# The residual's rounding, squaring and low part, one unit later in the output projection of a decoder step

## The chip, the cores and the metric

The kernel runs on one core of one Trainium2 chip. The metric is the device time of one launch in microseconds (us). Before the change it is 1759.76 us, the median of three runs (1758.87 to 1760.71 us).

## What is computed

The reference is one layer of a hybrid decoder for a prompt of 1024 tokens and 8 single-token requests, 1032 tokens in all. The change lies in its tail:

```python
def finish(x, ret_y, nsa_y, w_o, ln_post_mix, ln_pre_ffn, w_up, w_down, ln_post_ffn):
    mix = jnp.concatenate([ret_y, nsa_y], -1) @ w_o
    h = x + rmsnorm(mix, ln_post_mix)
    f = jnp.square(jax.nn.relu(rmsnorm(h, ln_pre_ffn) @ w_up)) @ w_down
    return h + rmsnorm(f, ln_post_ffn)
```

All tensors are float32. Features lie on the 128 partitions (8 tiles of features, `kt`), tokens in the free dimension, in three chunks of 344.

## The kernel before, in words

**Products in three parts.** Each float32 operand of a large product is split into a rounded part (`hi`, made by ScalarE with a copy) and the rest (`lo`, made by VectorE with a subtraction). A product is then three matmuls: hi by hi, hi by lo, lo by hi.

**Units.** `stage_tail` begins with 42 units, numbered `u`. The first 24 are the output projection `w_o`: for each of three token chunks, eight output tiles. The next 18 are the first part of `w_up`: six output tiles for each chunk. One unit is 24 matmuls of 128x344 at L2414, and writes one of three PSUM banks. Its weights (512 KB) come by a DMA that SyncE issues (L2232), `round_hi` on ScalarE makes `tail_hi` (L2534), and `reduce_lo` on VectorE makes `tail_lo` (L2753). Two buffers hold the split weights, so the rounding for unit u+1 waits until TensorE has finished unit u-1.

**What follows a chunk.** While the units of the next chunk run, the finished chunk goes through the rest of `h` and the start of the second norm. `place_of(u)` gives the chunk `k` and the slot `j` (0 to 7) for that side work. Slots 1 and 2 turn the chunk's sums of squares into a factor per token. From slot 2 on, feature tiles are taken as this table says:

```python
        SLOT_KT = {2: (0, 1), 3: (2, 3), 4: (4,), 5: (5,), 6: (6, 7), 7: ()}
```

For each feature tile, in this order:
- TensorE turns the tile of `x` into feature order (`turn_x`, three small matmuls at L2362), before the unit's own matmuls. It waits until the residual two tiles back has been added, because two PSUM banks hold the turned tiles.
- VectorE scales the projection (L2804) and adds the turned `x` (L2808). This is `residual`, and its result is `h`, in the tile `mixed_then_h`.
- GpSimd issues a DMA that stores the tile of `h` (L2283).
- ScalarE rounds `h` times the norm's gain into `act_hi` (L2572) and squares `h` into one of five buffers `h_squares` (L2575). Both are `normed_hi`.
- VectorE makes the low part `act_lo` (L2813, `normed_lo`), which needs `act_hi`.

TensorE adds up four squares at a time (`sum_h`, L2351): tiles 0 to 3 in slot 5 of the same chunk, tiles 4 to 7 in slot 1 of the next.

**The order on each engine** is written out by hand as one loop over `u` per engine, and each engine runs its instructions in that order. For one unit:
- ScalarE: `round_hi(u + 1)`; the side work of slots 1 to 3; the square and the copy of unit u-1's result (L2547, L2548), or the square of the `w_up` result (L2552); `normed_hi` for the slot's tiles; `scale_x`, a scaling of an earlier chunk's `h` (L2583), in units 16 to 27 and 32 to 35.
- VectorE: `reduce_lo(u + 1)`; the side work; the sum of squares of unit u-1 (L2769), or, ahead of `reduce_lo`, the relu of the `w_up` result (L2777); `residual` for the slot's tiles; `normed_lo` for the same tiles.
- SyncE: the weight loads in order, and behind each from unit 28 on the store of a `w_up` result.

After the 42 units TensorE runs the rest of the feed-forward layer (L2469 and L2519), to the end of the kernel.

Of the kernel before, what the change touches and what calls it, by code (L numbers as in the profile page):

```python
# [1914 lines left out]
def stage_tail(nc, m, ps, io, h_rows, f_forms, f_last):  # L1915
# [6 lines left out]
    with Stage(nc, "tail") as ctx:  # L1922
# [110 lines left out]
        SLOT_KT = {2: (0, 1), 3: (2, 3), 4: (4,), 5: (5,), 6: (6, 7), 7: ()}  # L2033
# [15 lines left out]
        def place_of(u):  # L2049

            if KT <= u < 4 * KT:
                return u // KT - 1, u % KT
            if 4 * KT <= u < NU:
                return 3, u - 4 * KT + 1
            return None, None

        def y_place_of(u):
            return (u // KT - 1, u % KT) if u >= KT else (None, None)
# [274 lines left out]
        def _(pe):  # L2333
            ones = m.c("ones")

            def token_totals(sums, at):

                for j in range(4):
                    last = pe.matmul(ps[0:SUB, 6, at + j:at + j + 1], sums[:, j * SUB:(j + 1) * SUB], ones[:, 0:1], start=True, stop=True,  # L2339
                                     skip_group_check=True)  # L2340
                return last

            def spread_out(out, d):
                return pe.matmul(out, ones[0:SUB, :], d[:].rearrange("p a n -> p (a n)"), start=True, stop=True, skip_group_check=True)

            def sum_h(grp):
                pe.wait_ge(h_squared, 4 * grp + 4)
                if grp % 2 == 0 and grp:
                    pe.wait_ge(h_copied, grp // 2)
                for i in range(4):  # L2350
                    last = pe.matmul(ps[32 * i:32 * i + 32, 7, 0:TN], ones[:, 0:32], hsq[(4 * grp + i) % 5][:], start=(grp % 2 == 0),  # L2351
                                     stop=(grp % 2 == 1), skip_group_check=True)
                last.then_inc(h_summed, 1)

            def turn_x(c, kt):
                g = KT * c + kt
                if kt == 0:
                    pe.wait_ge(x_loaded[c], 48 if c == 2 else 32)
                if g >= 2:
                    pe.wait_ge(h_ready, g - 1)  # L2360
                for t, n in enumerate(PIECES):
                    last = pe.transpose(ps[:, 3 + g % 2, t * P:t * P + n], x[X_SLOT[c]][0:n, t, kt * P:(kt + 1) * P], m.c("ident")[0:n, 0:n])  # L2362
                last.then_inc(x_turned, 1)

            def behind_chunk(k, j):
                if j == 1:
                    if k < 3:
                        if k >= 2:
                            pe.wait_ge(rstd_ready, k - 1)
                        pe.wait_ge(summed, 7 * (k + 1))  # L2370
                        token_totals(acc[k % 2], 0).then_inc(totals, 1)
                    if k:
                        sum_h(2 * k - 1)
                if j == 2:
                    if k < 3:
                        pe.wait_ge(diagonal, k + 1)
                        if k:
                            pe.wait_ge(normed, KT * k)
                        spread_out(ps[:, 5, 0:TN], diag).then_inc(spread, 1)
                    if k:  # L2380
                        pe.wait_ge(h_copied, k)
                        token_totals(h_part, 4).then_inc(h_totals, 1)
                if j == 3 and k:
                    pe.wait_ge(h_diagonal, k)
                    spread_out(ps[:, 6, 64:64 + TN], h_diag).then_inc(h_spread, 1)
                if k < 3:
                    if j == 5:
                        sum_h(2 * k)
                    for kt in SLOT_KT[j] if j >= 2 else ():
                        turn_x(k, kt)  # L2390

            for u, (what, n, c) in enumerate(tiles):
                k, j = place_of(u)
# [108 lines left out]
            for u in range(NL):  # L2502
                c, n = divmod(u, KT)
                k, j = y_place_of(u)
# [24 lines left out]
        def _(act):  # L2529
            def round_hi(p):  # L2530
                act.wait_ge(raw_loaded[raw_slot[p]], 16 * raw_use[p])
                if p >= 2:
                    act.wait_ge(unit_done, p - 1)
                act.activation(whi[p % 2][:], wraw[raw_slot[p]][:], ACT.Copy).then_inc(hi_ready, 1)  # L2534

            def split(n):
                c = n // 4
                for kts in mix_parts(n):
                    act.activation(m.hi[:, kts, chunk(c)], m.mixT[:, kts, chunk(c)], ACT.Copy).then_inc(mix_hi, 1)

            def evacuate(u):
                what, n, c = tiles[u]
                if what == "o":
                    act.wait_ge(unit_done, u + 1)
                    if n >= 3:
                        act.wait_ge(summed, 7 * c + n - 2)
                    act.activation(msq[n % 2][:] if n else acc[c % 2][:], ps[:, u % 3, 0:TN], ACT.Square).then_inc(squared, 1)  # L2547
                    act.activation(hT[:, n, chunk(c)], ps[:, u % 3, 0:TN], ACT.Copy).then_inc(o_evacuated, 1)  # L2548
                else:
                    k = u - NO  # L2550
                    act.wait_ge(evacuated, k + 1)
                    act.activation(f[k % 3][:], f[k % 3][:], ACT.Square).then_inc(f_squared, 1)  # L2552
# [24 lines left out]
            def scale_x(n):  # L2577

                c, kt = divmod(n, KT)
                act.wait_ge(n_lo, n + 1)  # L2580
                act.wait_ge(h_squared, n + 1)
                act.wait_ge(h_stored[c], 16 * KT)
                act.activation(hT[:, kt, chunk(c)], hT[:, kt, chunk(c)], ACT.Copy, scale=m.lnT[:, 16 + kt:17 + kt]).then_inc(scaled, 1)  # L2583
# [91 lines left out]
            for u in range(NU + 1):  # L2675
                if u in head_ends:
                    evacuate(u - 1)
                if u and u + 1 < NU:
                    round_hi(u + 1)
                k, j = place_of(u)  # L2680
                if k is not None:
                    behind_chunk(k, j)
                if u and u not in head_ends:
                    evacuate(u - 1)
                if u < 8:
                    split(4 + u)
                if k is not None and k < 3 and j >= 2:
                    for kt in SLOT_KT[j]:
                        normed_hi(k, kt)
                if 2 * KT <= u < NO:  # L2690
                    scale_x(u - 2 * KT)
                if NO <= u < NO + 4:
                    scale_x(KT + 2 * (u - NO))
                    scale_x(KT + 2 * (u - NO) + 1)
                if 4 * KT <= u < 4 * KT + 4:
                    for kt in X_SCALES[u - 4 * KT]:
                        scale_x(2 * KT + kt)
                if u in (38, 40):
                    x_hi_of((u - 38) // 2)
                if u == NU - 2:  # L2700
                    left_hi_of(0)
                if u == NU - 1:
                    for at in range(1, LEAD):
                        left_hi_of(at)
                if u == NU:
                    x_hi_of(2)
# [42 lines left out]
        def _(dve):  # L2749
# [260 lines left out]
            for u in range(NU + 1):  # L3010
                early = u in head_ends or u > NO + 1
                if early:
                    evacuate(u - 1)
                if u and u + 1 < NU:
                    reduce_lo(u + 1)
                k, j = place_of(u)
                if k is not None:
                    behind_chunk(k, j)
                if u and not early:
                    evacuate(u - 1)  # L3020
                if u < 8:
                    split(4 + u)
                if k is not None and k < 3 and j >= 2:
                    for kt in SLOT_KT[j]:
                        residual(k, kt)
                    for kt in SLOT_KT[j]:
                        normed_lo(k, kt)
                for n, q in X_PARTS.get(u, ()):
                    x_difference(n, q)
                if u == 39:  # L3030
                    first_sums()
                if u == 40:
                    x_lo_of(0, 0)
                    x_lo_of(0, 1)
                    left_lo_of(0)
                if u == NU - 1:
                    for at in range(1, LEAD):
                        left_lo_of(at)
                if u == NU:
                    x_lo_of(1, 0)  # L3040
                    x_lo_of(1, 1)
# [108 lines left out]
```

## Time and profile before

| | |
|---|---|
| median of three runs | 1759.76 us |
| the profiled execution's own time | 1759.33 us |
| its span in the trace | 1757.6 us |
| TensorE busy | 1637.6 us, 93% of the span |
| VectorE busy | 1063.5 us, 61% |
| ScalarE busy | 694.0 us, 39% |
| granted TensorE clock, mean | 0.975 |

The time of a run counts from launch to end, the span from the first to the last instruction in the trace; they differ by 1.7 us. The trace says for every instruction when it began, how long it took, and, in square brackets, how long its engine had stood idle before it and what ended that. Overlapping instructions of one engine are both shown in full, so the distance between two starts can be shorter than the duration.

### The profile page before, as it was taken

What the parts mean: (1) busy time and instruction counts of PE and PEld (TensorE: products, weight loads), DVE (VectorE), ACT (ScalarE), POOL (GpSimd) and SP (SyncE); (2) the same over time, 40 slices, a digit from 0 to 9 for tenths busy, and PEclk for the clock granted to TensorE, in tenths of its full rate; (3) what the DMA queues carried; (4) which work ended last, traced back from release to release, by engine and by line L of the source; (5) the groups of instructions that cost most, each with busy time, mean ns of one, the idle gap of its engine ahead of it and who ended that gap; (6) DMA issues with size and microseconds to landing.
All of it is one profiled execution on the core that took longest, in us unless ns stands there. A gap on an engine that the chain in (4) does not pass through costs nothing. (4 is left out here: it accounts for less than half of the span.)

```text
span 1757.6 us, 31453 instructions
## 1 busy us (share of the span) xinstructions
PE 1637.6 (93%) x12256; PEld 1453.7 (83%) x12256; DVE 1063.5 (61%) x1841; ACT 694.0 (39%) x1270; POOL 212.9 (12%) x305
## 2 busy tenths in 40 slices
PE   4999999997889778999998989999999999999997
PEld 4989989897784566655556988999999999999997
DVE  5556352121115536777876666877776788787566
ACT  5223322211001127666655665633333453433343
POOL 1000000012533220000000110032222000000011
PEclk9999999999899889999999999999999999999998
DMA  8111111142885340000006546534343743543464
GB/s 303 49 38 50 37 50 40 29 120 82 221 223 169 113 132 1 1 1 0 1 1 172 151 138 190 155 121 151 133 145 139 277 170 127 187 146 121 126 173 159
DMA packets 206838, 204.05 MB, mean 116 GB/s; under 512 B 15325, under 2 KB 175666, under 8 KB 203106
## 3 DMA queue, kind: packets, MB, share of 16 engines
q1 hardware_dynamic: 170930, 154.33, 28.3%
q0 software_dynamic: 12720, 37.21, 6.9%
q10 hardware_dynamic: 23040, 10.50, 2.3%
q8 instruction: 98, 1.61, 0.4%
q14 instruction: 50, 0.41, 0.1%
HBM read 163.27 MB, written 42.89 MB: 117 GB/s over the span
## 5 line engine op out<-in xcount | busy, mean ns | idle before, releaser
L2469 PE MATMUL psum<-right_hi,left_hi 128*128 128x258 f32 x1088 | 307.6, 283 | 3.3 <-issue 2.8
L2469 PE MATMUL psum<-right_hi,left_lo 128*128 128x258 f32 x1088 | 307.4, 283 | 0.0
L2469 PE MATMUL psum<-right_lo,left_hi 128*128 128x258 f32 x1088 | 307.0, 282 | 0.0
L235 PE MATMUL psum<-act_hi,whi 128*128 128x344 f32 x648 | 213.4, 329 | 4.0 <-DVE act_lo L408 4.0
L2469 PEld LDWEIGHTS psum<-right_hi,left_hi 128*128 128x128 f32 x1088 | 205.6, 189 | 3.7 <-issue 2.9
L235 PE MATMUL psum<-act_hi,wlo 128*128 128x344 f32 x648 | 206.9, 319 | 0.0
L235 PE MATMUL psum<-act_lo,whi 128*128 128x344 f32 x648 | 206.8, 319 | 0.0
L2469 PEld LDWEIGHTS psum<-right_lo,left_hi 128*128 128x128 f32 x1088 | 205.7, 189 | 0.0
L2469 PEld LDWEIGHTS psum<-right_hi,left_lo 128*128 128x128 f32 x1088 | 205.6, 189 | 0.0
L235 PEld LDWEIGHTS psum<-act_hi,whi 128*128 128x128 f32 x648 | 121.8, 188 | 11.4 <-DVE act_lo L408 4.4
L235 PEld LDWEIGHTS psum<-act_lo,whi 128*128 128x128 f32 x648 | 121.8, 188 | 0.4
L235 PEld LDWEIGHTS psum<-act_hi,wlo 128*128 128x128 f32 x648 | 121.8, 188 | 0.0
L2414 PE MATMUL psum<-act_hi,tail_hi 128*128 128x344 f32 x328 | 107.1, 326 | 5.2 <-issue 5.2
L2612 ACT ACTIVATE left_hi<-down_weights 128x512 fp32r<-128x512 f32 x84 | 52.9, 632 | 133.9 <-PE psum L2469 130.7
L2414 PE MATMUL psum<-act_hi,tail_lo 128*128 128x344 f32 x328 | 104.8, 319 | 0.0
L2414 PE MATMUL psum<-act_lo,tail_hi 128*128 128x344 f32 x328 | 104.6, 319 | 0.0
L1738 ACT ACTIVATE att_pT<-psum 128x512 f32<-128x512 f32 (+2 forms) x152 | 76.0, 539 | 42.1 <-PE psum L1667 40.3
L1667 PE MATMUL psum<-const,att_p 128*128 128x128 f32 x528 | 76.8, 280 | 13.0 <-ACT att_pT L1738 12.1
L2469 PE MATMUL psum<-act_hi,left_lo 128*128 128x258 f32 x312 | 88.1, 282 | 0.0
L2469 PE MATMUL psum<-act_hi,left_hi 128*128 128x258 f32 x312 | 88.1, 282 | 0.0
L2469 PE MATMUL psum<-act_lo,left_hi 128*128 128x258 f32 x312 | 88.0, 282 | 0.0
L2854 DVE TENSOR_TENSOR left_lo<-down_weights,left_hi 128x512 fp32r<-128x512 f32 x84 | 57.8, 688 | 43.4 <-ACT left_hi L2612 43.4
(441 smaller groups left out, 3622.3 us busy)
## 6 DMA issues: line engine op xcount, KB each, us to landing
hidden_forms<-pair_out SPq DMA_DIRECT2D x84, 258.0 KB, 2.4
right_raw<-hidden_forms SPq DMA_DIRECT2D x21, 1032.0 KB, 5.0
wraw<-in_w_in SPq DMA_DIRECT2D x27, 512.0 KB, 3.7
pair_raw<-in_w_up SPq DMA_DIRECT2D x13, 1024.0 KB, 5.5
down_weights<-in_w_down SPq DMA_DIRECT2D x12, 1024.0 KB, 7.9
last_raw<-in_w_down SPq DMA_DIRECT2D x24, 512.0 KB, 3.9
tail_raw<-in_w_o SPq DMA_DIRECT2D x23, 512.0 KB, 4.5
tail_raw<-in_w_up SPq DMA_DIRECT2D x18, 512.0 KB, 4.5
```

Of the source, the lines that this page charges most:

```text
L235: last = pe.matmul(out, w[:, kt, :], x[:, kt, :], start=(kt == 0 and n == 0), stop=(kt == KT - 1 and n == 2))
L1667: last = pe.transpose(ps[:, 4 + n % 2, (x - a) * P:(x - a + 1) * P], p[k % 3][:, block_cols(i, x)], m.c("ident"))
L1738: act.activation(pT[(t // R) % 2][:, a:b, t % R, :], ps[:, 4 + n % 2, 0:(b - a) * P].rearrange("p (a n) -> p a n", n=P), ACT.Copy).then_in ...
L2414: last = pe.matmul(ps[:, u % 3, 0:TN], wt[:, kt, :], xt[:, kt, cols], start=(kt == 0 and i == 0), stop=(kt == KT - 1 and i == 2))
L2469: last = pe.matmul(ps[:, first_bank(at) + e, 0:HT // 2], wt[:, kt, :], xt[:, kt, cols], start=(opens and kt == 0 and i == 0), stop=(kt == ...
L2612: act.activation(left_hi[at % SLOTS][:], left_source(at), ACT.Copy).then_inc(form_hi, 1)
L2854: dve.tensor_tensor(left_lo[at % SLOTS][:], left_source(at), left_hi[at % SLOTS][:].bitcast(F32), ALU.subtract).then_inc(form_lo, 1)
```

## The change

Three engines' loops are touched. In the chunk's side work `normed_hi` on ScalarE and `normed_lo` on VectorE take the tiles of the slot before (slot j handles `SLOT_KT[j - 1]`), so each follows its tile's `residual` by one unit. `residual` stays where it is. On TensorE the first `sum_h` of a chunk moves from slot 5 to slot 6. No instruction is added or removed, and no DMA is moved.

```diff
@@ block.tensor, behind_chunk
                 if k < 3:
-                    if j == 5:
+                    if j == 6:
                         sum_h(2 * k)
                     for kt in SLOT_KT[j] if j >= 2 else ():
                         turn_x(k, kt)
@@ block.scalar
                 if u < 8:
                     split(4 + u)
-                if k is not None and k < 3 and j >= 2:
-                    for kt in SLOT_KT[j]:
+                if k is not None and k < 3 and j >= 3:
+                    for kt in SLOT_KT[j - 1]:
                         normed_hi(k, kt)
@@ block.vector
                 if k is not None and k < 3 and j >= 2:
                     for kt in SLOT_KT[j]:
                         residual(k, kt)
-                    for kt in SLOT_KT[j]:
+                    for kt in SLOT_KT[j - 1] if j > 2 else ():
                         normed_lo(k, kt)
```

ScalarE, first chunk, from slot 2 into slot 3 (`tail_hi` is the rounded weight of the next unit; a minus is a row that stood there before, a plus one that stands there now):

```order
 L2547 ACTIVATE mix_squares_13194<-psum 128x344
 L2548 ACTIVATE mixed_then_h<-psum 128x344
-L2572 ACTIVATE act_hi<-mixed_then_h,lnT 128x344
-L2575 ACTIVATE h_squares_13179<-mixed_then_h 128x344
-L2572 ACTIVATE act_hi<-mixed_then_h,lnT 128x344
-L2575 ACTIVATE h_squares_13180<-mixed_then_h 128x344
 L2534 ACTIVATE tail_hi_13189<-tail_raw_13185 128x1024
 L2547 ACTIVATE mix_squares_13193<-psum 128x344
 L2548 ACTIVATE mixed_then_h<-psum 128x344
 L2572 ACTIVATE act_hi<-mixed_then_h,lnT 128x344
+L2575 ACTIVATE h_squares_13179<-mixed_then_h 128x344
+L2572 ACTIVATE act_hi<-mixed_then_h,lnT 128x344
```

The four instructions that need `h` of this slot stood ahead of the next weight's rounding; now the rounding and the evacuation of one more unit come first.

VectorE, second chunk, from the last residual of slot 2 to the end of slot 3. Before:

```order
L2808 TENSOR_TENSOR mixed_then_h<-mixed_then_h,psum 128x344
L2813 SCALAR_TENSOR_TENSOR act_lo<-mixed_then_h,lnT,act_hi 128x344 x2
L2753 TENSOR_TENSOR tail_lo_13191<-tail_raw_13185,tail_hi_13189 128x1024
L2769 TENSOR_TENSOR mix_square_sums_13195<-mix_square_sums_13195,mix_squares_13193 128x344
L2804 SCALAR_TENSOR_TENSOR mixed_then_h<-mixed_then_h,lnT,psum 128x344
L2808 TENSOR_TENSOR mixed_then_h<-mixed_then_h,psum 128x344
L2804 SCALAR_TENSOR_TENSOR mixed_then_h<-mixed_then_h,lnT,psum 128x344
L2808 TENSOR_TENSOR mixed_then_h<-mixed_then_h,psum 128x344
L2813 SCALAR_TENSOR_TENSOR act_lo<-mixed_then_h,lnT,act_hi 128x344 x2
```

With the change:

```order
L2808 TENSOR_TENSOR mixed_then_h<-mixed_then_h,psum 128x344
L2753 TENSOR_TENSOR tail_lo_13191<-tail_raw_13185,tail_hi_13189 128x1024
L2769 TENSOR_TENSOR mix_square_sums_13195<-mix_square_sums_13195,mix_squares_13193 128x344
L2804 SCALAR_TENSOR_TENSOR mixed_then_h<-mixed_then_h,lnT,psum 128x344
L2808 TENSOR_TENSOR mixed_then_h<-mixed_then_h,psum 128x344
L2804 SCALAR_TENSOR_TENSOR mixed_then_h<-mixed_then_h,lnT,psum 128x344
L2808 TENSOR_TENSOR mixed_then_h<-mixed_then_h,psum 128x344
L2813 SCALAR_TENSOR_TENSOR act_lo<-mixed_then_h,lnT,act_hi 128x344 x2
```

The pair of low parts ahead of `tail_lo` is gone from this place; the pair at the end is now that of slot 2. The totals per chunk are the same.

## Rows read from the trace of the kernel before

**Rows 1.** Busy time by stretch, the numbers from the start of the span

```profile
core 0: us, PE busy (x) PEld busy (x) DVE busy (x) ACT busy (x) POOL busy (x), PEclk, DMA share, GB/s
984.00:1104.00 120.00, 111.01 (x744) 103.35 (x743) 81.58 (x136) 72.25 (x142) 14.87 (x27) 1.00 0.54 162
1104.00:1134.00 30.00, 30.00 (x193) 30.00 (x192) 25.51 (x30) 17.46 (x25) 0.00 (x0) 1.00 0.51 148
1500.00:1700.00 200.00, 200.00 (x1559) 199.78 (x1558) 146.37 (x196) 78.97 (x93) 8.08 (x15) 1.00 0.46 149
```

**Rows 2.** Who waited for whom, 984 to 1104 us: total, times, longest

```profile
DVE tail_lo L2753 <- ACT tail_hi L2534: 31.0, 23, 3.6
ACT act_hi L2572 <- DVE mixed_then_h L2808: 29.6, 15, 2.2
...
PE psum L2362 <- DVE mixed_then_h L2808: 6.1, 7, 1.8
ACT tail_hi L2534 <- DMA tail_raw<-in_w_up: 5.7, 3, 2.8
...
PE psum L2414 <- issue: 2.9, 2, 1.9
```

**Rows 3.** ScalarE's timeline: start, duration, instruction, idle time before it

```profile
1039.08 0.58 ACT L2572 ACTIVATE act_hi<-mixed_then_h,lnT 128x344 fp32r<-128x344 f32 x1 [2.14 <-DVE mixed_then_h L2808]
1039.57 0.48 ACT L2575 ACTIVATE h_squares<-mixed_then_h 128x344 f32<-128x344 f32 x1
1039.95 0.57 ACT L2583 ACTIVATE mixed_then_h<-mixed_then_h,lnT 128x344 f32<-128x344 f32 x1
1040.42 1.04 ACT L2534 ACTIVATE tail_hi<-tail_raw 128x1024 fp32r<-128x1024 f32 x1
1041.37 0.43 ACT L2547 ACTIVATE mix_squares<-psum 128x344 f32<-128x344 f32 x1
1041.71 0.44 ACT L2548 ACTIVATE mixed_then_h<-psum 128x344 f32<-128x344 f32 x1
1044.28 0.58 ACT L2572 ACTIVATE act_hi<-mixed_then_h,lnT 128x344 fp32r<-128x344 f32 x1 [2.13 <-DVE mixed_then_h L2808]
```

**Rows 4.** VectorE's timeline in the same unit

```profile
1041.57 1.23 DVE L2753 TENSOR_TENSOR tail_lo<-tail_raw,tail_hi 128x1024 fp32r<-128x1024 f32 x1 [1.29 <-ACT tail_hi L2534]
1042.71 0.51 DVE L2769 TENSOR_TENSOR mix_square_sums<-mix_square_sums,mix_squares 128x344 f32<-128x344 f32 x1
1043.13 0.56 DVE L2804 SCALAR_TENSOR_TENSOR mixed_then_h<-mixed_then_h,lnT,psum 128x344 f32<-128x344 f32 x1
1043.73 0.51 DVE L2808 TENSOR_TENSOR mixed_then_h<-mixed_then_h,psum 128x344 f32<-128x344 f32 x1
1044.90 0.58 DVE L2813 SCALAR_TENSOR_TENSOR act_lo<-mixed_then_h,lnT,act_hi 128x344 fp32r<-128x344 f32 x1 [0.65 <-ACT act_hi L2572]
```

**Rows 5.** TensorE's timeline around a slot boundary without a wait

```profile
983.90 0.40 PE L2414 MATMUL psum<-act_hi,tail_hi 128*128 128x344 f32 x1
...
987.75 0.76 PE L2362 MATMUL psum<-const,x_rows_again 128*128 128x128 f32 x6
988.30 0.41 PE L2414 MATMUL psum<-act_hi,tail_hi 128*128 128x344 f32 x1
```

**Rows 6.** TensorE's timeline at the two longest waits of the stretch

```profile
1042.00 0.46 PE L2362 MATMUL psum<-const,x_rows_again 128*128 128x128 f32 x3
1044.30 0.52 PE L2362 MATMUL psum<-const,x_rows_again 128*128 128x128 f32 x3 [1.85 <-DVE mixed_then_h L2808]
1044.61 0.41 PE L2414 MATMUL psum<-act_hi,tail_hi 128*128 128x344 f32 x1
...
1054.32 0.39 PE L2414 MATMUL psum<-act_hi,tail_hi 128*128 128x344 f32 x1 [1.93 <-issue]
```

**Rows 7.** DMA issues by line, 1054 to 1134 us: KB each, median us to landing

```profile
tail_raw<-in_w_up SPq DMA_DIRECT2D x16, 512.0 KB, 4.5
```

**Rows 8.** The slowest landing of a `w_up` tile: SyncE's issue, ScalarE's rounding

```profile
1089.36 0.37 SPq L2232 DMA_DIRECT2D tail_raw<-in_w_up  x1
...
1095.40 1.06 ACT L2534 ACTIVATE tail_hi<-tail_raw 128x1024 fp32r<-128x1024 f32 x1 [1.69 <-DMA tail_raw<-in_w_up]
```

**Rows 9.** TensorE's waits from 1134 us to the end

```profile
PE psum L2481 <- DVE mlp_out L3004: 4.6, 2, 3.8
PE psum L2469 <- issue: 2.8, 1, 2.8
PE psum L2339 <- DVE y_square_sums L2984: 1.7, 1, 1.7
PE psum L2469 <- DVE pair_out L2918: 0.6, 1, 0.6
```

## The prediction, as put on record before the changed kernel ran

> **What bounds the kernel now.** I read the busy times by stretch first. From 1104 us to 1700 us TensorE hardly pauses, and the last such stretch has it busy for all of 200.00 us [rows 1]. Where TensorE is the bound, only time that TensorE gives up can be won. The stretch of the change, 984 to 1104 us, is different: TensorE is busy for 111.01 of 120.00 us, at a granted clock of 1.00, the 2.4 GHz level. VectorE (81.58 us) and ScalarE (72.25 us) have more than a quarter of it free [rows 1]. So about 9 us of TensorE idle time lie here, while no engine is full.
>
> The waits name the cause [rows 2]. TensorE waited 7 times for a residual (6.1 us) and twice for a split weight (shown as "issue", 2.9 us): 9.0 us in nine waits. In the same stretch VectorE waited 31.0 us for ScalarE's rounded weight, and ScalarE 29.6 us for VectorE's residual. Two engines that wait for each other that long, both unfilled, run in a ring.
>
> The timelines show the ring's length for a slot with one feature tile in the second chunk: from one `act_hi` at 1039.08 us to the next at 1044.28 us, 5.20 us [rows 3]. In it ScalarE rounds `h`, squares, scales, rounds the next weight at 1040.42 us; only then may VectorE start that weight's low part, at 1041.57 us, then the sum of squares and the two steps of the residual, from 1043.13 to 1044.24 us [rows 4]; and that residual releases the next `act_hi`. TensorE needs less: a unit takes 3.85 us from its first matmul to the next instruction, and six turning matmuls (two tiles) 0.55 us [rows 5], so about 4.1 us with one tile and 4.4 us with two. TensorE has a lead when a chunk begins, uses it up over the slots at about 1 us per slot, and then stands still.
>
> **The change, part by part.**
>
> *ScalarE.* `normed_hi` of a slot moves behind the next unit's rounding. It then asks for a residual that VectorE finished a unit ago, so the ring is cut: the rounding of the next weight waits only for the unit that frees its buffer, and no longer for this slot's residual. Cost in ScalarE time: none, the same instructions run. A slot with two tiles takes, from start to start [rows 3], 0.95 for the weight, 0.34 + 0.34 for the evacuation, 2 x (0.49 + 0.38) and 0.47 for the scaling: 3.84 us, under TensorE's 4.4. This holds in the first two chunks; in the third two scalings fall in early slots, and one relu square replaces the evacuation, about the same sum.
>
> *VectorE.* The low parts follow a unit later too and find `act_hi` ready, so the 0.65 us gap in front of them [rows 4] goes. The fullest slot is 3: 1.14 for the weight, 0.42 for the sum, two residuals of 1.03 each (0.60 + 0.43), two low parts. The trace of before shows a low part's duration, 0.58 us [rows 4]; its spacing lies between 0.42, the shortest here, and 0.58. I take 0.49, that of the equally long `act_hi` [rows 3]. Sum: 1.14 + 0.42 + 2.06 + 0.98 = 4.6 us against TensorE's 4.4. The 0.2 us are recovered in slot 4: 1.14 + 0.42 + 1.03 + 0.98 = 3.6 against 4.1. Over slots 2 to 7 it is 6 x 1.56 + 8 x 1.03 + 8 x 0.49 = 21.5 us, against at least 6 x 3.85 + 8 x 0.27 = 25.3 us on TensorE. VectorE does not become the bound.
>
> *TensorE.* The first four squares arrive a unit later; `sum_h` moves with them, from slot 5 to 6. The work is the same, so it costs nothing; it also gives slot 6's turning matmuls, which wait for the residuals of slots 4 and 5, a little more time.
>
> *What is late next.* The weight for unit u+1 can be rounded when unit u-1 ends. Rounding, a semaphore, low part: 1.04 + 0.1 + 1.23 = 2.4 us [rows 3, 4], and TensorE wants it 3.85 us after the unit's start: 1.4 us to spare. The second residual of a two-tile slot ends about 2.3 + 0.4 + 2.1 = 4.8 us after the unit before has ended. The next slot's second turning matmuls want it after 3.85 + 0.27 = 4.1 us, plus what TensorE does between the two units (0.55 us of turning, and more in slots 1 to 3, where the factors per token are spread): 4.7 us or later. That is even, within 0.2 us. It is the one tight place, at the step from slot 2 to 3. Per chunk it may cost nothing, or up to 0.5 us if VectorE starts late; I take 0.1, near the low end because the first chunk before already shows this step with no wait [rows 5], so 0.3 us in all.
>
> *DMA, SyncE and GpSimd.* Nothing is moved on them, but TensorE passes faster, so the same loads must land in less time. `w_up` weights have two raw buffers: low part done, load lands (4.5 us median) [rows 7], round, low part: 4.5 + 2.4 = 6.9 us for two units, against 7.7 us or more on TensorE. They stay hidden, and cost nothing; the slowest landing, 6.0 us from 1089.36 to 1095.40 us [rows 8], makes 8.4 us once, which the 1.4 us of slack covers. If all landed that late, the cover would be gone (a rival below). Residual stores keep their place behind the residuals; GpSimd waits for those alone.
>
> **The sum.** Each of nine waits costs more than its idle time, because an unhindered matmul starts before the one ahead has ended. At the longest of them the first turning started at 1042.00 us; unhindered the second would start 0.27 us later and the unit at 1042.55 us, after 0.55 us [rows 5]. The unit started at 1044.61 us [rows 6]: 2.06 us for 1.85 us of idle time, 0.2 more. So 9.0 + 9 x 0.2 = 10.8 us is what TensorE gives up. Less 0.3 us for the tight place: **10.5 us**. It lies on the path: behind 1104 us TensorE is the bound, and what releases its later waits [rows 9] is itself started by TensorE's products, so all of it moves forward together. The profiled execution took 1759.33 us, 0.43 below the median: 1759.33 - 10.5 = 1748.8 us by its own time, and **1749.3 us** as a median.
>
> **The rivals.**
>
> *VectorE's two-tile slots bind* (gain 6.5 to 9 us, chance 0.10). If low parts don't overlap their neighbours, each full slot grows. By durations alone slot 3 is 1.23 + 0.51 + 2 x (0.56 + 0.51) + 2 x 0.58 = 5.0 us against 4.4, so 0.6 us late in three chunks, and some of it again in slot 6: 2 to 4 us back, about 1752 us. Against it: the sum at 1042.71 us lasts 0.51 us and the next instruction starts at 1043.13 us, 0.42 later [rows 4]. The Trainium skill, "VectorE: DVE Perf Modes", section on the DRAIN, says that the next operation does not start until the pipe is empty, and adds that one that isn't held starts earlier; here the trace sides with the addition. By the strict rule the time would be this rival's.
>
> *Landings of `w_up` lengthen* (gain 3 to 8 us, chance 0.09). At 6.0 us for every load the two-buffer round is 8.4 us against about 8.0 us of TensorE: 8 rounds by 0.4 us, 3 us back, 1752.5 us. For it: three waits of ScalarE for them, 5.7 us [rows 2]. Against: between 1104 and 1134 us eight units run without any TensorE idle time [rows 1], at the full rate that the change would bring earlier.
>
> *The same, past its tipping point: slower* (chance 0.03). With landings of 7.7 us a round is 10.1 us against 8.0; 8 rounds lose 17 us, less 1.4 of slack, more than the 10.8 won: some 1764 us. It decides from about 7.2 us. No `w_up` tile took over 6.0 us, and the stretch moves 162 GB/s at a DMA share of 0.54 [rows 1].
>
> *The gain does not reach the end* (within 0.2%, chance 0.05). Either ScalarE still has to wait for the residual inside its loop, or a later stage waits for something not tied to TensorE, and takes the time back: 1757 to 1760 us. Against the first: the order of ScalarE's instructions as listed. Against the second: all later waits are 9.7 us in five places [rows 9], released by engines that TensorE's results start.
>
> **How the numbers follow.** 0.73 for the forecast (gain 9 to 11.5 us). A measurement of this kernel tells a difference from 0.2%, 3.5 us. Faster by more than that: 0.73 + 0.10 + 0.09 = 0.92; same 0.05; slower 0.03. The likeliest case spans 1748.3 (the tight place free) to 1751; the range goes down to 1747.3 for a downstream wait that closes and the spread of the runs (0.9 us to either side), and up to 1753.3 to take in both rivals that cost part of the gain.
>
> **What the profile after would show.** ScalarE's idle time before L2572 falls from 29.6 us to under 3 us, and its waits before L2534 are for TensorE (that is health, the buffer is the limit). VectorE's wait for L2534 moves from the ring to the same cause. TensorE's idle time between unit 10 and unit 34 falls from 9.0 us to under 1 us, and unit 34 starts about 10.5 us earlier; what is left stands at slot 3, before L2362. The stages after 1134 us keep their lengths. I am wrong if TensorE still waits for L2808 for more than 2 us in sum, if ScalarE's wait for `tail_raw` grows past 10 us and reaches TensorE, or if the span shrinks by less than the start of unit 34 (the first after the last side work) moves.

## The result, and the profile after

| | before | changed | ratio, 95% interval |
|---|---|---|---|
| median, us (runs) | 1762.49 (6) | 1751.19 (6) | 0.9941, 0.9925 to 0.9957 |
| lowest to highest, us | 1758.87 to 1768.86 | 1747.43 to 1754.48 | |
| span of the profiled execution, us | 1757.6 | 1745.8 | |
| TensorE busy, share of the span | 93% | 94% | |

The changed kernel is 0.59% faster: by the ratio 10.4 us of 1762.49, with 7.6 and 13.2 us as the ends of the interval. Three more runs of before, taken beside it, are in its median now, which is therefore 2.7 us above the 1759.76 us of the first three. The profiled execution of the changed kernel took 1747.43 us, the fastest of its six. The ratios below leave out two executions in a slow state, one of the kernel before (2614.54 us) and one of the kernel with the later sum alone (2273.16 us).

What matters is one stretch. The busy times of the changed kernel by stretch: first from the start of unit 10 to the first matmul of the products (L2469), which is the whole stretch that the change can reach, then three stretches that answer to [rows 1]. Columns: stretch, its length, busy time of PE, PEld, DVE, ACT and POOL, granted clock, DMA share, GB/s.

```profile
982.34:1121.36 139.02, 139.02 (x936) 133.49 (x933) 105.88 (x165) 88.78 (x166) 14.86 (x27) 1.00 0.57 172
984.00:1092.00 108.00, 108.00 (x737) 102.47 (x737) 79.49 (x135) 71.08 (x140) 14.86 (x27) 1.00 0.60 182
1092.00:1122.00 30.00, 30.00 (x194) 30.00 (x194) 25.68 (x30) 17.46 (x25) 0.00 (x0) 1.00 0.49 145
1488.00:1688.00 200.00, 200.00 (x1561) 199.77 (x1560) 146.37 (x195) 78.75 (x92) 8.08 (x15) 1.00 0.46 148
```

The whole stretch in the kernel before:

```profile
983.90:1133.91 150.01, 141.02 (x935) 133.36 (x933) 107.00 (x165) 89.71 (x166) 14.87 (x27) 1.00 0.54 159
```

TensorE now never stops in it: busy for 139.02 of 139.02 us, where it was busy for 141.02 of 150.01. The stretch is 10.99 us shorter: 8.99 us of idle time, and 2.00 us of busy time, with the same matmuls and the same granted clock. The last row, in the stage of the products, agrees with that of [rows 1] to two matmuls in 1559: nothing changed there.

The waits of the changed kernel, 984 to 1092 us, which answer to [rows 2] (who waited for whom, total, times, longest):

```profile
ACT tail_hi L2534 <- PE psum L2414: 29.4, 21, 3.2
DVE tail_lo L2753 <- ACT tail_hi L2534: 20.4, 22, 3.0
```

ScalarE's 29.6 us for the residual (`act_hi <- DVE mixed_then_h`) are gone altogether, and so are all waits of TensorE and the 5.7 us for `w_up` loads. In their place ScalarE waits for TensorE to free a weight buffer, and VectorE for ScalarE: the order of who waits for whom now ends at the engine that bounds the kernel.

**Where the 11.8 us between the two profiled spans come from.** I cut both spans at the same two instructions.

| stretch | before | after | won |
|---|---|---|---|
| start to unit 10 (nothing of it is changed) | 983.90 | 982.34 | 1.56 |
| unit 10 to the first matmul of the products | 150.01 | 139.02 | 10.99 |
| of it unit 10 to unit 34 | 119.57 | 108.58 | 10.99 |
| products to the end | 623.69 | 624.44 | -0.75 |

The outer two rows are what an execution happens to bring (below); the middle one is the change. All of it was won by unit 34. So the experiments are judged by that stretch, beside their times: it is the sharper measure. Its limit is that each kernel has one trace. The two kernels below whose change wins nothing took 149.01 and 150.51 us for it, where the kernel before took 150.01, so a difference of 1 us against the kernel before says little.

### The profile page after: what moved, and what is told of

It reads as the page before. It is cut to its first block and busy times, and to the rows that moved or that the text cites. A ratio compares the mean times of both kernels' runs of the same rounds, so it can differ in the third digit from the quotient of the medians.

```text
span 1745.8 us, 31453 instructions
## 1 busy us (share of the span) xinstructions
PE 1634.9 (94%) x12256; PEld 1445.0 (83%) x12256; DVE 1062.7 (61%) x1841; ACT 692.7 (40%) x1270; POOL 213.5 (12%) x305
## 5 line engine op out<-in xcount | busy, mean ns | idle before, releaser
L2469 PE MATMUL psum<-right_hi,left_hi 128*128 128x258 f32 x1088 | 308.2, 283 | 3.3 <-issue 2.7
L2469 PE MATMUL psum<-right_hi,left_lo 128*128 128x258 f32 x1088 | 308.0, 283 | 0.0
L2469 PE MATMUL psum<-right_lo,left_hi 128*128 128x258 f32 x1088 | 307.7, 283 | 0.0
L2469 PEld LDWEIGHTS psum<-right_hi,left_hi 128*128 128x128 f32 x1088 | 206.3, 190 | 3.7 <-issue 2.9
L2469 PEld LDWEIGHTS psum<-right_lo,left_hi 128*128 128x128 f32 x1088 | 206.4, 190 | 0.0
L2469 PEld LDWEIGHTS psum<-right_hi,left_lo 128*128 128x128 f32 x1088 | 206.4, 190 | 0.0
L1738 ACT ACTIVATE att_pT<-psum 128x512 f32<-128x512 f32 (+2 forms) x152 | 76.0, 539 | 40.1 <-PE psum L1667 38.1
L1667 PE MATMUL psum<-const,att_p 128*128 128x128 f32 x528 | 76.6, 279 | 12.7 <-ACT att_pT L1738 11.8
L2469 PE MATMUL psum<-act_hi,left_lo 128*128 128x258 f32 x312 | 88.1, 282 | 0.0
L2469 PE MATMUL psum<-act_hi,left_hi 128*128 128x258 f32 x312 | 88.1, 282 | 0.0
L2469 PE MATMUL psum<-act_lo,left_hi 128*128 128x258 f32 x312 | 88.0, 282 | 0.0
```

The lines of the kernel that those rows point to most:

```text
L1667: last = pe.transpose(ps[:, 4 + n % 2, (x - a) * P:(x - a + 1) * P], p[k % 3][:, block_cols(i, x)], m.c("ident"))
L1738: act.activation(pT[(t // R) % 2][:, a:b, t % R, :], ps[:, 4 + n % 2, 0:(b - a) * P].rearrange("p (a n) -> p a n", n=P), ACT.Copy).then_in ...
L2469: last = pe.matmul(ps[:, first_bank(at) + e, 0:HT // 2], wt[:, kt, :], xt[:, kt, cols], start=(opens and kt == 0 and i == 0), stop=(kt == ...
```

## The experiments

**My theory:** ScalarE and VectorE wait for each other in a ring that passes through the residual, `act_hi`, the squares, the next weight's rounding and its low part. Only what takes a link out of the ring wins time; cutting it wins all of it, and then neither engine is near its limit. **Rivals:** the low part's place on VectorE alone does it (it waited behind `act_hi`); the later sum on TensorE does it; VectorE is nearly full, and a little more work on it would give the gain back; the loads of `w_up` are nearly late.

### The low part alone

```
                     for kt in SLOT_KT[j]:
                         residual(k, kt)
-                    for kt in SLOT_KT[j]:
+                    for kt in SLOT_KT[j - 1] if j > 2 else ():
                         normed_lo(k, kt)
```

(against the kernel before)

> Only VectorE's low part follows one unit later; ScalarE still waits for the slot's residual before it rounds the next weight. The theory (a ring residual, act_hi, next weight's rounding, next weight's low part, residual) says that the low part is no link of the ring: no gain, within 0.1% of the kernel before, with the nine TensorE waits of 9.0 us in sum still there. The rival (VectorE's gap of 0.65 us in front of each low part is what holds TensorE up) says that up to 24 x 0.2 us go, 3 to 5 us faster.

Measured: 1763.49 us, ratio 1.0003 (0.9990 to 1.0015). Two waits of this kernel, 984 to 1104 us:

```profile
ACT act_hi L2572 <- DVE mixed_then_h L2808: 29.6, 15, 2.2
...
PE psum L2362 <- DVE mixed_then_h L2808: 5.3, 6, 1.9
```

ScalarE's wait for the residual is the same 29.6 us in 15 waits. VectorE no longer stands in front of the low part, but it only arrives earlier at the next weight, which ScalarE has not rounded yet. The stretch took 149.01 us, 1.00 less than before. The rows place this in the third chunk: its first load landed sooner, so that ScalarE waited for it 1.79 us instead of 2.84, and TensorE's waits there are 0.36 and 0.98 us instead of 0.25, 0.94 and 0.99. In the second chunk one wait was 0.40 us instead of 1.93, but TensorE had lost that time to a lower clock (last section). The low part is not in the ring, and its move alone is worth nothing.

### The later sum alone

```
-                    if j == 5:
+                    if j == 6:
                         sum_h(2 * k)
```

(against the kernel before)

> Only the first sum of squares moves from slot 5 to slot 6 on TensorE. Theory: within 0.1% of the kernel before; the waits for residuals stay at about 6 us, perhaps placed a slot otherwise, since 0.72 us of work moves past slot 5 and 6. Rival (the later squares sum is itself worth something): 0.5 to 2 us faster.

Measured: 1762.66 us, ratio 1.0001 (0.9988 to 1.0014); the stretch took 150.51 us against 150.01. The wait for the residual stands at 29.6 us in 15 waits once more. TensorE's idle time is 7.7 us instead of 9.0, but behind a stop of 1.92 us its clock fell for a while (last section), and the stretch is no shorter. No gain, no loss.

### Rounding, squares and low part later, the sum left where it was

```
-                    if j == 6:
+                    if j == 5:
                         sum_h(2 * k)
```

(against the changed kernel)

> Rounding, squares and low part one unit later, but the first sum of squares stays in slot 5. Theory: the squares of tiles 2 and 3 are ready in slot 4, so the sum in slot 5 doesn't wait; the whole gain stays, 10 to 11 us against the kernel before and within 0.1% of the full change. Rival (the sum must move for the rest to pay): TensorE waits for the squares before L2351, 0.5 to 1 us per chunk, so 1.5 to 3 us of the gain are missing.

Measured: 1752.62 us, ratio 0.9943 (0.9926 to 0.9960). The stretch:

```profile
986.90:1125.91 139.01, 139.01 (x936) 133.48 (x934) 105.86 (x165) 88.91 (x166) 14.92 (x27) 1.00 0.58 172
```

139.01 us and no idle time on TensorE: the whole gain, without the sum's move. The squares come a unit later now, but the fourth is there in time for slot 5's place too.

### Only the squares later: the ring shortened, not cut

```
                 if k is not None and k < 3 and j >= 3:
                     for kt in SLOT_KT[j - 1]:
+                        square_h(k, kt)
+                if k is not None and k < 3 and j >= 2:
+                    for kt in SLOT_KT[j]:
                         normed_hi(k, kt)
```

(against the changed kernel; `square_h` is the squaring taken out of `normed_hi`; the low part is back in its own slot, the sum stays in slot 6)

> Only the squares (L2575) follow one unit later, ahead of the slot's act_hi, and the sum of squares moves to slot 6; act_hi and low part stay in their slot. Theory: the ring is shortened by one link, 0.38 us for each feature tile, and not cut; over eight tiles of a chunk that is 3 us, more than chunks 1 and 3 lose and less than chunk 2 does. Worked out over the slots: about 5 us faster than before, half of the full change. Rival (what matters is only that ScalarE waits for the residual at all): no gain, or under 1 us.

Measured: 1757.90 us, ratio 0.9976 (0.9966 to 0.9987), about 4.2 us. The stretch, and its waits for the residual and on TensorE:

```profile
984.19:1128.30 144.11, 140.78 (x936) 133.35 (x934) 106.99 (x165) 90.05 (x166) 14.92 (x27) 1.00 0.56 166
```

```profile
ACT act_hi L2572 <- DVE mixed_then_h L2814: 26.3, 24, 2.2
...
PE psum L2414 <- issue: 1.7, 3, 1.2
PE psum L2362 <- DVE mixed_then_h L2814: 1.4, 2, 1.1
```

5.90 us were won of 10.99. ScalarE's timeline shows the shorter ring. The square of the tile before (L2578 here) fills a place where ScalarE would stand anyway, and behind `act_hi` the scaling follows at once:

```profile
1039.30 0.48 ACT L2578 ACTIVATE h_squares<-mixed_then_h 128x344 f32<-128x344 f32 x1
1041.54 0.58 ACT L2572 ACTIVATE act_hi<-mixed_then_h,lnT 128x344 fp32r<-128x344 f32 x1 [1.76 <-DVE mixed_then_h L2814]
1042.03 0.57 ACT L2586 ACTIVATE mixed_then_h<-mixed_then_h,lnT 128x344 f32<-128x344 f32 x1
1042.51 1.04 ACT L2534 ACTIVATE tail_hi<-tail_raw 128x1024 fp32r<-128x1024 f32 x1
```

From `act_hi` to the rounding of the weight it is 0.97 us, where [rows 3] have 1.34 (1039.08 to 1040.42). A link of 0.38 us taken out of a slot with one tile, twice that in one with two, gave back over half of what the ring cost. That is the ring's own signature: its length decides, and not how busy an engine is. (ScalarE's busy time in the stretch, 90.05 us, is even a little above before's 89.71.)

### The change in the second chunk alone

```
-                    for kt in SLOT_KT[j]:
+                    for kt in SLOT_KT[j] if k != 1 else SLOT_KT[j - 1] if j > 2 else ():
                         normed_hi(k, kt)
```

(against the kernel before; `normed_lo` likewise, and the sum in slot 6 for this chunk)

> The full change in the second chunk alone; the first and third are as before. Theory: the waits are a matter of each chunk by itself, so what TensorE gives up there goes, 4.5 us of idle time in three waits and 0.2 us for each: about 5 us faster than before, and the 4.5 us of waits of the other two chunks stay. Rival (a chunk's lead is handed on, so that one cured chunk also helps the next, or is eaten by it): 7 us or more, or 3 us or less.

Measured: 1756.83 us, ratio 0.9968 (0.9957 to 0.9979), about 5.6 us. The stretch, and what TensorE still waited for:

```profile
984.01:1127.78 143.77, 140.15 (x935) 133.43 (x934) 106.48 (x164) 89.15 (x166) 14.87 (x27) 1.00 0.57 166
```

```profile
PE psum L2362 <- DVE mixed_then_h L2808: 2.6, 4, 1.0
PE psum L2414 <- issue: 1.0, 1, 1.0
```

6.24 us were won. By TensorE's waits the second chunk held 4.53 us of idle time before (0.75 + 1.85 + 1.93), the first 2.29 and the third 2.18. Left are 2.29 in the first, as before, and 1.33 in the third. So the second chunk's three waits are gone, and the third chunk lost one of its own (0.85 us in all). That fourth wait is not clearly the cure's: the kernel with the low part alone, whose second chunk was not cured, has nearly the same two waits left in the third (0.36 and 0.98 us; here 0.35 and 0.98). There ScalarE waited 1.05 us less for the third chunk's first load, here not at all. Idle time removed: 4.53 + 0.85 = 5.38 us; the other 0.86 us for four waits is again 0.2 us for each. The second chunk by itself is worth 4.53 us and 0.2 us for each of three waits, 5.2 us, which is what the theory said.

### Every low part made twice: how much room has VectorE?

```
                 dve.wait_ge(n_hi, KT * c + kt + 1)
+                dve.wait_ge(spare_done, KT * c + kt)
+                dve.scalar_tensor_tensor(spare[:], hT[:, kt, cols], m.lnT[:, 16 + kt:17 + kt], m.hi[:, kt, cols].bitcast(F32),
+                                         ALU.mult, ALU.subtract).then_inc(spare_done, 1)
```

(against the changed kernel; the spare copy is read by nobody)

> The full change, and VectorE makes each low part of h twice, the first time into a spare tile that nobody reads: about 0.5 us more VectorE work for each of 24 feature tiles, 12 us in all. Theory: VectorE has room in every slot but the fullest, so that of the 12 us only about 1 us reaches TensorE: within 0.1% of the changed kernel. Rival (VectorE's two-tile slots are at the edge, as the 0.2 us of the prediction's tight place would have it): each of the two-tile slots 3 and 7 passes on 0.5 to 1 us, 3 to 6 us slower than the changed kernel.

Measured: 1753.65 us, ratio 0.9946 (0.9928 to 0.9964). The stretch, and TensorE's only wait in it:

```profile
989.60:1129.17 139.57, 139.25 (x936) 133.51 (x933) 116.38 (x189) 89.25 (x166) 14.92 (x27) 1.00 0.58 171
```

```profile
1007.72 0.52 PE L2363 MATMUL psum<-const,x_rows_again 128*128 128x128 f32 x3 [0.33 <-DVE mixed_then_h L2809]
```

VectorE does 10.5 us more (116.38 against 105.88) and the stretch is 0.55 us longer. The wait is at the second turning of slot 6 in the first chunk, which needs slot 5's residual: with four low parts in slot 3 and four in slot 4, VectorE falls behind, runs packed from 994.87 us on, and is late two slots on. In the changed kernel this residual ended at 998.81 us, 1.1 us before its turning (998.30 + 0.51, against 999.62 + 0.27). VectorE's timeline of slot 4 here also shows the spacing of the low parts in a packed row:

```profile
1003.04 0.57 DVE L2815 SCALAR_TENSOR_TENSOR spare_low_part<-mixed_then_h,lnT,act_hi 128x344 fp32r<-128x344 f32 x1
1003.53 0.57 DVE L2817 SCALAR_TENSOR_TENSOR act_lo<-mixed_then_h,lnT,act_hi 128x344 fp32r<-128x344 f32 x1
1004.02 0.57 DVE L2815 SCALAR_TENSOR_TENSOR spare_low_part<-mixed_then_h,lnT,act_hi 128x344 fp32r<-128x344 f32 x1
```

Each lasts 0.57 us and the next starts 0.49 later. The rival that VectorE binds falls: with four low parts in a full slot, two more than the change has, TensorE stands for 0.33 us once. The stretch decides this, and not the times: the median is 2.5 us above the changed kernel's, and the intervals of both reach further than that. Without the doubled parts VectorE has room in the slots that have low parts; the step from slot 2 to 3 is not loaded by this experiment.

### Each `w_up` load later: how much room have the loads?

```
+                if p >= NO + 2:
+                    sp.wait_ge(unit_done, p - 2)
```

(in SyncE's weight loader, ahead of the load of weight p; against the changed kernel. The second version has `p - 1`.)

> The full change, and each w_up load from the third on is issued only when TensorE has finished the unit three before it, about 1.5 us later than now. The load then has to land and be split within two units, 7.7 us or more, less nothing: 4.5 + 2.4 = 6.9 us. Theory: still hidden, 0 to 2 us slower than the changed kernel, the loss at the landings that take 5.5 us or more. Rival (the loads are at their limit already): each of 16 units gives up 0.5 us or more, over 8 us.

Measured: 1753.32 us, ratio 0.9945 (0.9929 to 0.9960). The stretch, and ScalarE's wait for the loads in it:

```profile
988.89:1128.21 139.32, 139.32 (x936) 133.48 (x934) 105.43 (x164) 88.16 (x165) 14.87 (x27) 1.00 0.58 172
```

```profile
ACT tail_hi L2536 <- DMA tail_raw<-in_w_up: 18.0, 11, 2.7
```

ScalarE stands for 18.0 us behind loads, three times as long as in the kernel before [rows 2], and TensorE feels nothing: no idle time, 0.30 us in all. This waiting takes the place of waiting for TensorE (40.1 us in the changed kernel's whole stretch, 23.5 here), so it is spare time. Counted from unit 10, the 16 loads were issued 0.6 to 3.2 us later than in the changed kernel, 1.9 us in the mean.

> The full change, and each w_up load from the third on is issued only when TensorE has finished the unit two before it. Landing and splitting, 4.5 + 2.4 = 6.9 us or more, then stand against a single unit of 3.85 us: 3 us lost in each of 16 units, less the slots' side work. Theory: 28 to 45 us slower than the changed kernel. Rival (landings get shorter when they don't share the DMA engines with stores): under 20 us.

Measured: 1795.40 us, ratio 1.0180 (1.0156 to 1.0205), 44 us more than the changed kernel. The stretch, ScalarE's wait for the loads, and TensorE's timeline at two stops that follow each other:

```profile
985.73:1171.10 185.37, 158.86 (x935) 150.85 (x934) 107.52 (x167) 89.41 (x167) 14.86 (x27) 0.88 0.44 130
```

```profile
ACT tail_hi L2536 <- DMA tail_raw<-in_w_up: 67.3, 15, 8.4
```

```profile
1133.85 0.62 PE L2416 MATMUL psum<-act_hi,tail_hi 128*128 128x344 f32 x1 [3.39 <-issue]
...
1147.41 0.62 PE L2416 MATMUL psum<-act_hi,tail_hi 128*128 128x344 f32 x1 [3.35 <-issue]
```

One unit of delay more, and the loads are in a ring with TensorE: it stops once in two units, which take 13.56 us (1133.85 to 1147.41) where two units of the late part take 7.6 us undisturbed. Of the 46.35 us that the stretch grew, 26.5 are idle time, in eight stops of 2.7 to 4.0 us; 19.8 are busy time, at the granted clock of 0.88 over the stretch. The expectation's 28 to 45 us held 44 us, but in part by luck: it counted idle time alone and had no term for the clock. Behind a stop of 3.6 us the clock is at the lower level, 1.2 GHz and a little over (the busy times again, the clock stands behind POOL's):

```profile
1120.00:1126.00 6.00, 6.00 (x23) 5.76 (x22) 2.99 (x4) 2.72 (x5) 0.00 (x0) 0.54 0.01 2
```

The rival of late loads exists, and past its tipping point it is dearer than the rival in the prediction said, whose price of 17 us had no term for the clock. The point lies between the two delays: 1.9 us later costs 0.3 us, a unit more costs 44.

## Why the prediction was right, point by point

Forecast 1749.3 us (1747.3 to 1753.3), measured 1751.19 us. The gain was forecast as 10.5 us, against a median of 1759.76; it measured 10.4 us by the ratio (7.6 to 13.2) and 10.99 us by the stretch. The median lies 1.9 us above the forecast, though the gain was no smaller: the same kernel before has a median 2.7 us higher in the larger set of runs.

**The ring: shown.** It had to be ScalarE's wait for the residual that ties the two engines together. Cutting it without the later sum brings 11.00 us, all of it; shortening it by the squares brings 5.90 us, cutting it in one chunk 6.24 us; moving what lies outside it brings nothing (ratios 1.0003 and 1.0001).

**9.0 us of idle time: right.** All nine waits went: 8.99 us.

**0.2 us on top of each wait: right, 0.22 measured.** 2.00 us of TensorE's busy time went with nine waits. It is not work: a matmul that follows one without a gap starts before that one has ended, and after a stop this overlap is missing.

**0.3 us for the tight place: did not occur.** This was the sum's only term that failed; the other 0.2 us between 10.5 and 10.99 are nine times 0.22 instead of 0.2. The second residual of slot 2 and the second turning of slot 3, in the second chunk, from the timelines of VectorE and TensorE in the changed kernel:

```profile
1022.56 0.51 DVE L2808 TENSOR_TENSOR mixed_then_h<-mixed_then_h,psum 128x344 f32<-128x344 f32 x1
...
1027.48 1.06 DVE L2813 SCALAR_TENSOR_TENSOR act_lo<-mixed_then_h,lnT,act_hi 128x344 fp32r<-128x344 f32 x2
1028.84 1.23 DVE L2753 TENSOR_TENSOR tail_lo<-tail_raw,tail_hi 128x1024 fp32r<-128x1024 f32 x1 [0.31 <-ACT tail_hi L2534]
```

```profile
1023.01 0.76 PE L2362 MATMUL psum<-const,x_rows_again 128*128 128x128 f32 x6
1023.56 0.40 PE L2414 MATMUL psum<-act_hi,tail_hi 128*128 128x344 f32 x1
```

The residual ends at 1022.56 + 0.51 = 1023.07 us; the six turning matmuls start at 1023.01, so the second three start at about 1023.28. The margin is 0.2 us, and 0.1 us in the first chunk (985.86 + 0.51 = 986.37, against 986.19 + 0.27 = 986.46): "even, within 0.2 us" was right, and it fell on the good side in all three chunks. That it did so by 0.1 us is luck as much as reckoning. No experiment loads this place: slot 2 has no low part, so the doubled low parts only come behind it.

**A low part's spacing of 0.49 us: right.** Two of them together take 1.06 us in the row above: 0.49 and then one of 0.57. The Trainium skill, "VectorE: DVE Perf Modes", section on the DRAIN, has the next operation wait for an empty pipe unless it isn't held; by the rows the next one starts 0.08 us before the last one's end, here and in the kernel with doubled low parts. By the strict rule the prediction had 2 to 4 us given back, and none were.

**ScalarE's slot with two tiles, 3.84 us: 3.92 measured.** Its timeline in the changed kernel, second chunk, from one weight to the next:

```profile
1027.68 1.06 ACT L2534 ACTIVATE tail_hi<-tail_raw 128x1024 fp32r<-128x1024 f32 x1 [0.73 <-PE psum L2414]
1028.65 0.44 ACT L2547 ACTIVATE mix_squares<-psum 128x344 f32<-128x344 f32 x1
1028.98 0.45 ACT L2548 ACTIVATE mixed_then_h<-psum 128x344 f32<-128x344 f32 x1
1029.32 0.58 ACT L2572 ACTIVATE act_hi<-mixed_then_h,lnT 128x344 fp32r<-128x344 f32 x1
1029.79 0.49 ACT L2575 ACTIVATE h_squares<-mixed_then_h 128x344 f32<-128x344 f32 x1
1030.17 0.58 ACT L2572 ACTIVATE act_hi<-mixed_then_h,lnT 128x344 fp32r<-128x344 f32 x1
1030.65 0.48 ACT L2575 ACTIVATE h_squares<-mixed_then_h 128x344 f32<-128x344 f32 x1
1031.03 0.57 ACT L2583 ACTIVATE mixed_then_h<-mixed_then_h,lnT 128x344 f32<-128x344 f32 x1
1031.78 1.06 ACT L2534 ACTIVATE tail_hi<-tail_raw 128x1024 fp32r<-128x1024 f32 x1 [0.18 <-PE psum L2414]
```

Compare it with [rows 3]: there ScalarE stood for 2.1 us ahead of each `act_hi`; here it doesn't stand there at all, and both its stops are ahead of the weight, for TensorE. From 1027.68 to 1031.78 it is 4.10 us, less the 0.18 of waiting 3.92: the last scaling counts with its whole 0.57, since nothing follows it at once.

**Loads stay hidden: shown, with more room than I gave them.** ScalarE has no wait for `w_up` from 984 to 1092 us, and the 16 loads have the median of 4.5 us to landing that they had [rows 7], though the stretch moves 182 GB/s instead of 162. Part of this room is probably new, though no experiment separates it: the rounding no longer waits for the residual, and the raw buffer comes free 2.4 us behind the rounding's start, as before (1045.65 to 1048.07 us for one weight; 1054.62 to 1057.05 us for the same one in the kernel before).

**Nothing is taken back later: shown.** TensorE's waits of the changed kernel behind 1120 us, against [rows 9]:

```profile
PE psum L2481 <- DVE mlp_out L3004: 4.6, 2, 3.8
PE psum L2469 <- issue: 2.7, 1, 2.7
PE psum L2339 <- DVE y_square_sums L2984: 1.7, 1, 1.7
PE psum L2469 <- DVE pair_out L2918: 0.6, 1, 0.6
```

The same four, one of them 0.1 us shorter: they hang on TensorE's own products, and move with them. One of the prediction's signs of being wrong did show, taken at its word: the span shrank by 11.8 us, less than unit 34 moved, 12.55 us (1103.47 to 1090.92). The 0.75 us between them are the last row of the stretches' table. That part of the program took 623.6 to 628.2 us in the ten traces, so they lie within its scatter, and none of TensorE's waits there grew.

One form of the change was not tried: `normed_hi` a unit later with `normed_lo` left in its slot. By the loops as written the program would stand still, in the third chunk. VectorE would wait in one unit's turn for an `act_hi` that ScalarE makes in the next, behind the square of a `w_up` result; that square needs VectorE's relu, which stands behind VectorE's wait. In the first two chunks, where ScalarE's evacuation needs no relu, it would only be late. So the two moves go together, and no run shows ScalarE's move without VectorE's; that the low part's move is not what cuts the ring is shown by the run that has it alone.

## What to carry to other kernels

When two engines that each have a quarter of their time free wait for each other by about the same sum, look for a ring through their hand-written queues, and compare its length with the time that the bounding engine needs for one round; what the bounding engine waits is the difference, once its lead is used up. Let the consumer ask for last round's result and the ring is cut for nothing, as long as the buffers hold one round more; a link taken out pays in part, and moving what lies outside the ring has no effect. Count 0.2 us more than the idle time for each stop of TensorE that goes, and measure between two instructions of the bounding engine that enclose the change: here this gave 10.99 and 139.01 to 139.02 us, where the runs alone scatter by 7 to 10 us.

## What the runs showed of the hardware that I had not expected

**A short stop can cost clock, and not every time.** In the kernel with the low part alone, the same wait as in [rows 6], 1.86 us long, left the clock at the lower level. TensorE's timeline there:

```profile
1047.50 0.52 PE L2362 MATMUL psum<-const,x_rows_again 128*128 128x128 f32 x3 [1.86 <-DVE mixed_then_h L2808]
1047.80 0.44 PE L2414 MATMUL psum<-act_hi,tail_hi 128*128 128x344 f32 x1
...
1048.33 0.49 PE L2414 MATMUL psum<-act_hi,tail_lo 128*128 128x344 f32 x1
1048.62 0.49 PE L2414 MATMUL psum<-act_hi,tail_hi 128*128 128x344 f32 x1
```

Matmuls start 0.28 to 0.29 us apart, against 0.16 in the rows ahead of the stop. Busy times and granted clock just behind the stop, in this kernel:

```profile
1048.00:1052.00 4.00, 4.00 (x18) 4.00 (x17) 2.04 (x3) 2.55 (x6) 0.28 (x1) 0.57 0.11 44
```

and in the kernel before at the same place, behind its 1.85 us:

```profile
1044.80:1048.80 4.00, 4.00 (x28) 4.00 (x27) 2.61 (x4) 2.55 (x6) 0.28 (x1) 1.00 0.11 44
```

18 matmuls against 28 in 4 us. It cost little there, because the ring was the bound: the next wait was 0.40 us instead of 1.93. The kernel with the later sum alone shows the same behind its stop of 1.92 us:

```profile
1057.70:1062.00 4.30, 4.26 (x17) 4.29 (x18) 2.11 (x3) 2.34 (x5) 0.00 (x0) 0.60 0.71 204
```

The kernel before had stops of 1.85 and 1.93 us in its trace and kept the clock at 1.00 behind both. So stops of this length carry a risk that the 0.2 us do not count, and an execution of the kernel before that meets it should gain more from the change than these traces show.

**The outer parts of the program scatter more than the change's own stretch.** Unit 10 started between 982.34 and 989.60 us in the profiled executions, with the same code ahead of it, and the part from the products to the end took 623.6 to 628.2 us. One place where executions differ is 440 to 700 us: the granted clock there was 0.88 in the kernel before and 0.90 in the changed one. It does not explain the whole: the latest start of unit 10, 989.60 us, has 0.89 there. What sets the clock in that stage was not tried.
